# An fp32 kernel of two model blocks on one core: another order and other copies in its up projection, and norm sums in column groups

## What is computed

```
def rms_norm(x, g):
    xf = x.astype(jnp.float32)
    y = xf * lax.rsqrt(jnp.mean(xf * xf, axis=-1, keepdims=True) + EPS)
    return (y * g.astype(jnp.float32)).astype(x.dtype)
...
def conv_ffn(h, w_up, conv_w, w_down):
    a = dwconv_centred(h @ w_up, conv_w)
    val, gate = jnp.split(a, 2, axis=-1)
    return (val * jax.nn.silu(gate)) @ w_down
```

## Time and profile before

| what | value |
|---|---|
| median of 3 runs | 2653.74 us (2653.2 to 2656.26) |
| the profiled execution | 2656.84 us |
| its span | 2655.0 us |
| TensorE, matmuls | 2576.1 us, 97% |
| VectorE | 1068.6 us, 40% |
| ScalarE | 571.6 us, 22% |
| GpSimd | 176.3 us, 7% |
| up stage of layer 0 | from 1744.09 us on |
| up stage of layer 1 | from 2410.60 us on |

### The profile page before, as it was taken

The page is one execution under the profiler, slowest core; times in us unless marked ns, Lnnn a source line. Parts: engine busy times, 40 slices in busy tenths (PEclk is TensorE's granted clock), DMA queues, the critical chain, the costliest instruction groups (busy, mean ns, idle before and its releaser), DMA issues.

```text
span 2655.0 us, 31317 instructions
## 1 busy us (share of the span) xinstructions
PE 2576.1 (97%) x12702; PEld 1862.7 (70%) x12702; DVE 1068.6 (40%) x1883; ACT 571.6 (22%) x1105; POOL 176.3 (7%) x138
## 2 busy tenths in 40 slices
PE   7999999999999899899999999999999999998999
PEld 3556656656666577666886444778886687888998
DVE  2245365364464613254126111146664014115961
ACT  3122222122121112143124100121111013112211
POOL 0000000000000100000000000022120000003410
PEclk9999999999999999999999999999999999999999
DMA  8443343343323043212420222133233232344662
GB/s 313 159 163 133 115 142 112 131 163 116 126 96 111 29 122 95 62 40 73 111 90 7 64 63 63 64 96 95 80 102 88 65 80 64 110 143 129 174 173 66
DMA packets 319738, 280.58 MB, mean 106 GB/s; under 512 B 27618, under 2 KB 298602, under 8 KB 319514
## 3 DMA queue, kind: packets, MB, share of 16 engines
q1 hardware_dynamic: 317882, 274.89, 33.7%
q0 software_dynamic: 1280, 4.20, 0.4%
q10 hardware_dynamic: 479, 0.13, 0.0%
HBM read 278.15 MB, written 1.05 MB: 105 GB/s over the span
## 4 chain that ended last, share of the span: by engine, by line
PE 89%; DVE 7%; ACT 2%; issue 1%; DMA 1%; SPq 1%; ACTq 0%; DVEq 0%
PE ps L683 17%; PE ps L1254 11%; PE ps L1185 9%; PE ps L1323 4%; PE ps L692 4%; PE ps L1313 4%; PE ps L730 4%; PE ps L1197 3%; PE ps L1221 3%; PE ps L449 2%; PE ps L879 2%; PE ps L830 2%; PE ps L812 2%; DVE arena L2085 2%; PE ps L396 2%; PE ps L1034 2%
## 5 line engine op out<-in xcount | busy, mean ns | idle before, releaser
L683 PE MATMUL ps<-hT,ring_mem 128*128 128x512 f32 x1024 | 455.5, 598 | 1.7 <-ACT hT L462 1.7
L683 PEld LDWEIGHTS ps<-hT,ring_mem 128*128 128x128 f32 x1024 | 191.1, 191 | 234.8 <-issue 232.2
L1185 PE MATMUL ps<-hT,ring_mem 128*128 128x512 f32 (+1 forms) x768 | 250.3, 486 | 0.0
L1185 PEld LDWEIGHTS ps<-hT,ring_mem 128*128 128x128 f32 x768 | 145.9, 190 | 101.3 <-issue 91.4
L1254 PE MATMUL ps<-arena 128*128 128x256 f32 (+1 forms) x704 | 132.9, 333 | 12.4 <-DVE arena L2044 12.4
L2016 DVE TENSOR_TENSOR arena<-ps,arena 128x512 f32<-128x512 f32 (+1 forms) x48 | 26.8, 558 | 291.3 <-PE ps L1197 291.3
L730 PEld LDWEIGHTS ps<-arena,K_c 128*128 128x128 f32 x896 | 117.4, 196 | 32.6 <-issue 20.1
L1254 PE MATMUL ps<-hT,arena 128*128 128x256 f32 (+1 forms) x704 | 131.5, 330 | 0.0
L730 PE MATMUL ps<-arena,K_c 128*128 128x128 f32 x896 | 121.4, 291 | 7.4 <-ACT K_c L1467 7.4
L1254 PEld LDWEIGHTS ps<-arena 128*128 128x128 f32 x704 | 112.0, 195 | 22.4 <-issue 13.0
L1254 PE MATMUL ps<-hT,ring_mem 128*128 128x256 f32 (+1 forms) x704 | 123.6, 329 | 2.8 <-DMA ring_mem<-in_w_up_dram 2.8
...
## 6 DMA issues: line engine op xcount, KB each, us to landing
...
ring_mem<-in_hg_w_out_dram SPq DMA_DIRECT2D x8, 1024.0 KB, 12.1
```

The lines of the kernel that those rows point to most:

```text
L683: mm = PE.matmul(bank, wj[:, k, m * 128:m * 128 + 128], hT[:, k, :], start=k == 0, stop=k == 7)
L1185: mm = PE.matmul(ps[:, j, 0:n], wj[:, k, m * 128:m * 128 + 128], hT[:, k, c0:T], start=k == 0, stop=k == 7)
```

## The change

1. **Norm sums in column groups.** For thirteen norms `quarters_tensor` takes the place of `norm_tensor`: eight matmuls with a 128 x 32 matrix of ones, tile k into PSUM partitions 32 x (k mod 4) on. ScalarE copies the four partial sums to `root`, and `whole_tensor`, one matmul with the 128 x 128 matrix of ones some matmuls later, adds them (the factor under the root is 32 instead of 1, since each partial sum stands there 32 times).
2. **Two banks a strip.** The seven products of a strip share two banks: P2 is written where P1 was, P4 where P7 was, and P3 where P5 was, each after ScalarE has copied the earlier one out. Four strips can be in PSUM. ScalarE makes all these copies: P1, P7, P2, P5 (`up_first_scalar`, `seventh`, `second`, `fifth`).
3. **Another order on each engine.** TensorE: P1, P7, P2, P4, P5, P6, P3 in each strip; at the stage's start P1 of four strips around the norm sum, then P2 of four, then the rest in pairs. VectorE: `first_sum(f+1)`, `conv(f-1)`, `hidden(f-2)`, `gather(f)`, and gather has five operations, three of them with both inputs in SBUF.
4. **Weight sums.** VectorE makes one sum a strip instead of two, GpSimd three instead of two; the third is written in place in the ring.
5. **Slots.** Strip f lies in slot (f + 2) mod 4, so strips 0 and 1 lie in the words that the stage `out` doesn't use.
6. Banks of the stages around it are exchanged (`down` begins in banks 4 to 7), and one small operation of layer 1 (`nsink`) is left out.

```diff
...
+        QUARTERED = ["hg_post_a", "mla_pre_a", "hg_post_b", "mix0_a", "mla_post", "mix0_b", "ffn0_a", "ffn0_b", "mix1_a", "mix1_b",
+                     "ffn1_a", "ffn1_b", "final_a"]
+
...
+            if name in QUARTERED:
+                act.wait_ge(quarters_summed, QUARTERED.index(name) + 1)
+                act.wait_ge(normed, sq_base[name])
+                S.activation(root[:, at:at + n], stat(name, n), ACT.Copy).then_inc(quarters_kept, 1)
             act.wait_ge(stat_summed, norm_no[name] + 1)
             if norm_no[name]:
                 act.wait_ge(normed, sq_base[name])
-            S.activation(root[:, at:at + n], stat(name, n), ACT.Sqrt, bias=eps, scale=8.0 / k_n).then_inc(root_ready, 1)
+            S.activation(root[:, at:at + n], stat(name, n), ACT.Sqrt, bias=eps, scale=32.0 if name in QUARTERED else 8.0 / k_n).then_inc(root_ready, 1)
+
+        def quarters_tensor(pe, name, sq, n):
+
+
+            pe.wait_ge(root_ready, norm_no[name])
+            for k in range(8):
+                pe.wait_ge(squared, sq_base[name] + k + 1)
+                c = k % 4 * 32
+                mm = PE.matmul(stat(name, n)[c:c + 32, :], ones[:, 0:32], sq(k), start=k < 4, stop=k >= 4)
+            mm.then_inc(quarters_summed, 1)
+
+        def whole_tensor(pe, name, n, at=0):
+            pe.wait_ge(quarters_kept, QUARTERED.index(name) + 1)
+            PE.matmul(stat(name, n), ones, root[:, at:at + n], start=True, stop=True).then_inc(stat_summed, 1)
 
         def norm_tensor(pe, name, sq, ones_, n):
             k_n = dict(NORMS)[name]
@@ -491,7 +516,7 @@
         mod_mem = ring_mem[:, 8192:12288].rearrange("p (k n) -> p k n", k=4)
...
+            def first(f):
+                ring.wait_loaded(pe, name, (f + 2) % 4, f // 4)
+                if f >= 4:
+                    pe.wait_ge(u_ready, base + f - 3)
+                elif f >= 2:
+                    pe.wait_ge(x_added, x_part(l, "out", "_b", (1, 5)[f - 2]))
+                product(up_bank(f, 0)[:, 0:hw], up_parts(l, f)[0], hT[:, 0:4, a], ready=lambda k: wait_h(pe, f"ffn{l}_a", k) if f == 0 else None
+                        ).then_inc(p1_full, 1)
+
+            def second(f):
+                if f == 0:
+                    wait_h(pe, f"ffn{l}_a", 7)
+                pe.wait_ge(p1_kept, base + f + 1)
+                product(up_bank(f, 0)[:, 0:hw], up_parts(l, f)[1], hT[:, 4:8, a]).then_inc(p2_full, 1)
+
+            def seventh(f):
+                if f >= 4:
+                    pe.wait_ge(c_ready, base + f - 3)
+                pe.wait_ge(third_sum_ready, base + f + 1)
                 if f == 0:
                     pe.wait_ge(turned_ready, 4 * l + 1)
-                product(f, "P7", sums[:, 2], T_up[:, 0])
-                if f == 0:
-                    pe.wait_ge(turned_ready, 4 * l + 2)
-                product(f, "P5", sums[:, 0], hT[:, 0:4, b])
-                pe.wait_ge(sums_ready, FT * l + f + 1)
-                if f == 0:
-                    pe.wait_ge(turned_ready, 4 * l + 3)
-                product(f, "P6", sums[:, 1], T_up[:, 1])
-                mm = product(f, "P3", sums[:, 3], hT[:, 4:8, b])
+                product(up_bank(f, 1)[:, hw:2 * hw], up_parts(l, f)[2], T_up[:, 0]).then_inc(p7_full, 1)
+
+            def others(f):
+                _, _, _, a22 = up_parts(l, f)
+                pe.wait_ge(p7_kept, base + f + 1)
                 if f == 0:
                     pe.wait_ge(turned_ready, 4 * l + 4)
-                    mm = p4()
-                strip_used(mm)
-
-            plain(0)
+                if f >= 2:
+                    pe.wait_ge(first_sum_ready, (FT - 2) * l + f - 1)
+                product(up_bank(f, 1)[:, hw:2 * hw], a22, T_up[:, 2])
+                product(up_bank(f, 1)[:, 0:hw], S_up[:, f % 2, 0], hT[:, 0:4, b]).then_inc(p5_full, 1)
+                pe.wait_ge(p2_kept, base + f + 1)
+                pe.wait_ge(sums_ready, base + f + 1)
+                product(up_bank(f, 0)[:, hw:2 * hw], S_up[:, f % 2, 1], T_up[:, 1]).then_inc(p6_full, 1)
+                pe.wait_ge(p5_kept, base + f + 1)
+                strip_used(product(up_bank(f, 1)[:, 0:hw], S_up[:, f % 2, 2], hT[:, 4:8, b]))
+
+            first(0)
+            first(1)
             ffn_norm_tensor(pe, l, "_b")
-            for f in range(FT):
-                if f == 0:
-                    plain(1)
-                    pe.wait_ge(root_ready, norm_no[f"ffn{l}_b"] + 1)
-                if f >= 2:
-                    plain(f)
-                summed(f)
+            first(2)
+            first(3)
+            whole_tensor(pe, f"ffn{l}_b", hw, at=hw)
+            for f in range(4):
+                second(f)
+            for f in (0, 2):
+                seventh(f)
+                seventh(f + 1)
+                others(f)
+                others(f + 1)
+            for f in range(4, FT):
+                first(f)
...
+
+            def second(f):
+                act.wait_ge(p2_full, base + f + 1)
+                if f >= 2:
+                    act.wait_ge(conv_ready, base + f - 1)
+                S.activation(C_up[f % 2][:, 0:hw], up_bank(f, 0)[:, 0:hw], ACT.Copy).then_inc(p2_kept, 1)
...
             for f in range(FT):
-                act.wait_ge(strips_used, ring.stages[f"up{l}"]["first"] + f + 1)
-                S.activation(P1_up[:, 0:n // 2], up_region(f, "P1", n // 2), ACT.Copy).then_inc(p1_kept, 1)
-                act.wait_ge(c_ready, FT * l + f + 1)
+                if f >= 4:
+                    up_first_scalar(act, l, f)
+                if f >= 1:
+                    taps(f - 1)
+                if f >= 4 or f % 2 == 0:
+                    seventh(f)
+                if f < 4 and f % 2 == 0:
+                    seventh(f + 1)
+                second(f)
                 if f >= 2:
-                    act.wait_ge(hid_ready, raised(FT * l + f - 1))
-                for part in range(2):
-                    S.activation(acc[:, f % 2 * 2 + part, 0:n], C_up[f % 2][:, part, 0:n], ACT.Identity,
-                                 scale=tap(l, 1, f, part)).then_inc(tap_ready, 1)
-                if f:
-                    gate(f - 1)
...
+            def first_sum(f):
+
+
+                _, _, a21, a22 = up_parts(l, f)
+                wait_strip_f(dve, l, f - 2)
+                ring.wait_loaded(dve, f"up{l}", (f + 2) % 4, f // 4)
+                V.tensor_tensor(S_up[:, f % 2, 0], a21, a22, ALU.add).then_inc(first_sum_ready, 1)
+
             def gather(f):
-                P = lambda which: up_region(f, which, hw)
-                U = lambda i: U_up[:, i, 0:hw]
-                C = C_up[f % 2]
-                dve.wait_ge(strips_used, ring.stages[f"up{l}"]["first"] + f + 1)
-                dve.wait_ge(p1_kept, FT * l + f + 1)
-                if f >= 2:
-                    dve.wait_ge(tap_ready, 2 * (FT * l + f - 1))
-                st.mark(V.tensor_tensor(U(0), P1_up[:, 0:hw], P("P6"), ALU.add))
-                V.tensor_tensor(C[:, 0, 0:hw], P1_up[:, 0:hw], P("P2"), ALU.add)
+                C, U, P57 = C_up[f % 2], P1_up[:, f % 4, 0:hw], P57_up[f % 2]
+                both = view(C, (hw, 2), (1, hw), at=hw)
+                dve.wait_ge(p1_kept, base + f + 1)
+                dve.wait_ge(p2_kept, base + f + 1)
+                V.tensor_tensor(C[:, 0:hw], C[:, 0:hw], U, ALU.add)
+                dve.wait_ge(p6_full, base + f + 1)
+                V.tensor_tensor(U, U, up_bank(f, 0)[:, hw:n], ALU.add).then_inc(u_ready, 1)
+                dve.wait_ge(u_ready, base + f + 1)
+                dve.wait_ge(p7_kept, base + f + 1)
+                dve.wait_ge(p5_kept, base + f + 1)
+                st.link(V.tensor_tensor(both, view(U, (0, 2), (1, hw)), view(P57, (hw, 2), (1, hw)), ALU.add))
+                st.mark(V.tensor_tensor(C[:, n + hw:2 * n], C[:, n:n + hw], P57[:, 0:hw], ALU.add))
+                wait_strip_f(dve, l, f)
                 st.settle()
-                st.mark(V.tensor_tensor(U(1), U(0), P("P7"), ALU.add))
-                st.mark(V.tensor_tensor(U(2), U(0), P("P5"), ALU.add))
-                st.settle()
...
+            for f in range(FT):
+                if 1 <= f < FT - 1:
+                    first_sum(f + 1)
+                if f >= 1:
                     conv(f - 1)
                 if f >= 2:
                     hidden(f - 2)
+                gather(f)
+            conv(FT - 1)
+            hidden(FT - 2)
+            hidden(FT - 1)
 
...
                 pool.wait_ge(y_ready, raised(8 * l + 8))
                 for f in range(FT):
-                    t, j = divmod(f, 4)
-                    ring.wait_loaded(pool, f"up{l}", j, t)
+                    ring.wait_loaded(pool, f"up{l}", (f + 2) % 4, f // 4)
                     sums = S_up[:, f % 2]
                     a11, a12, a21, a22 = up_parts(l, f)
                     if f >= 2:
-                        pool.wait_ge(first_sums_ready, (FT - 2) * l + f - 1)
+                        pool.wait_ge(first_sum_ready, (FT - 2) * l + f - 1)
```

(6 more changed lines are left out.)

222 lines of the change are left out of this document (124 added, 98 removed).

## The result

The changed kernel takes 2672.32 us (median of 4 runs, 2670.55 to 2674.73) against 2654.79 us (2653.2 to 2656.26) for the kernel before, measured beside it: ratio 1.0065, 95% interval 1.005 to 1.0079. The profiled execution's span is 2672.8 us against 2655.0.

The account below looks back on a forecast made before the run. TensorE, busy 97%, was taken as the bound, with VectorE nearly so in layer 1's up stage. Terms -12.8 - 3.2 + 35 = +19 gave 2673 us as a median; range 2642 to 2696, from the terms' bounds 2656 to 2696.

Parts of the forecast that it names:

- Turn of layer 1: Layer 1's up stage, steady state: a strip takes 8.0 us instead of 6.25, TensorE waiting 1.75 us in each; +33 over the strips.
- Its mechanism: VectorE operations with two SBUF inputs advance at about 21% of their speed while GpSimd runs its sums.
- rival 3: Full exclusion in layer 1's up stage: multiply-adds do nothing beside GpSimd, a turn of 8.7 us, total 2686 us; chance 0.15.
- Rival 1: GpSimd steals less or lies elsewhere: VectorE never slowed, a turn of 5.2 us, stage TensorE-bound, total 2626 us; chance 0.17.
- Start of layer 1: Start of layer 1's up stage: new waits 11.2 and 5 for the clock, against 11.3 and 0.9 that go; +4.
- Clock in the steady state: Layer 1's up stage: the clock may fall after waits of 1.75 us, TensorE's slack taking most up; +2 (0 to 13).
- End: End of layer 1's up stage: VectorE's backlog gone, so waits of 2.11 and 0.5 and 1.7 us of lower clock go; -4.3.
- Layer 0: Start of layer 0's up stage: shorter wait for turned tiles, new waits for the third sum; net -3.2 us (-6 to 0).
- Norms: Thirteen norms' sums of squares in column groups: 2.09 us saved per full norm; -12.8 us in sum, between -16 and -8.
- Rivals 1 and 2: Rival 1, and a second: half as much lost in layer 1's up stage (40% speed), total 2657 us; the second's chance 0.10.
- rival 4: Norms' column groups run one after another: +0.43 instead of -2.09 us a norm, total 2691 us; chance 0.03.

## Why the prediction was right, step by step

**Turn of layer 1: right.** 8.0 us forecast, 8.05 measured; from the first wait for L1728 to the last one, 2579.56 - 2442.57 = 137.0 us for 17 strips, 30.7 more than 17 x 6.25, against 29.8 forecast. The four multiply-adds "at 4 us and more": 4.56. The wait for L1728: 1.53. The first longer wait: 3.30, forecast 3.5. GpSimd busy 51.50 of 100 us.

**Its mechanism: right in the operations and the size, wrong in form.** The prediction spread the loss as a speed of 21% under GpSimd. In truth each GpSimd sum holds one VectorE operation. Multiply-adds one by one show it; this is the answer for line L2189 of the changed kernel (duration of one in ns, lowest, median, highest):

```profile
L2189 DVE SCALAR_TENSOR_TENSOR arena<-K_c,vecs,arena x24: 471/1362/1489, 2458.6 to 2543.1; 128x255 f32<-128x255 f32 x24
```

Three of four last about as long as a sum, the fourth its own 0.47 us. The kernel before had it already; asked for one by one between 2458 and 2544 us, its multiply-adds are not all a little slow. In the strip of the earlier trace rows the first takes 1.26 us, beside GpSimd's second sum, and the other three 0.47 to 0.48:

```profile
L2085 DVE SCALAR_TENSOR_TENSOR arena<-K_c,vecs,arena x28: 471/482/1268, 2457.4 to 2536.0; 128x255 f32<-128x255 f32 x28
```

That the two forms agree on the turn rests on the shape of this row of work; with halved sums, 8.1 to 8.3 us by the 21% against 7.82 measured, they don't. The Trainium skill (SBUF — State Buffer, "Summary: rules for kernel authors") says that where VectorE has two SBUF inputs and GpSimd reads SBUF, the second to issue "fully blocks until the first finishes". These rows agree with it, operation by operation. What rival 3 took from that rule, that VectorE does nothing at all while GpSimd has sums to make (8.7 us, 2686), doesn't follow: between two sums one VectorE operation gets in. (Rival 1's turn adds up to 5.3 us and not 5.2 with the 1.79 us of the earlier trace rows for the multiply-adds; nothing hangs on it.)

**Start of layer 1: too dear.** +4 forecast. The stage took 2583.23 - 2396.23 = 187.0 us against 152.5 before, +34.6; less 30.7 and 3.3 this leaves +0.6. The waits were 2.35, 1.69 and 5.22 (forecast 2.4, 2.4, 5.2), the small ones of 1.2 didn't come, and the lower clock cost about 2.5 us and not 5: 0.9 after the first wait, 1.6 after the third, none after the second.

**Clock in the steady state: +2 forecast, nothing came.** Behind the first longer wait, 3.30 us, the clock did fall (0.50 from 2444.60 to 2446.60), and three products took 2446.98 - 2442.57 = 4.41 us instead of 2.68; but TensorE's slack took it up, for the next strip's wait was missing (no gap before 2450.60). After waits of 1.5 to 1.7 us in every strip the granted clock was 1.00 from 2450 to 2550. The term was taken from a single wait of 2.11 us.

**End: right.** -4.3 forecast; layer 1's first half of down took 38.0 us instead of 42.3.

**Layer 0: right.** -3.2 forecast, -2.7 in the trace (275.8 against 278.5 us), with the waits of 1.39, 3.41 and 0.91 us where 1.4, 3.1 to 3.5 and 1.0 stood.

**Norms: over.** -12.8 forecast, -10.8 by the traces, -8 by the runs. The groups took 1.00 us and not 0.93, so a norm saves 2.0 us and not 2.09; four norms from mix0_a to ffn0_a brought 7.3 us for the 8.4 forecast. Block one gave back all of its norms' savings: its last waited stretch ends at 1037.63 instead of 1036.43, and 1.06 of these 1.2 us were there before the first norm (943.04 against 944.10, a difference between the two executions ahead of anything the change touches). The forecast had -0.7 there, with +2 for the clock. Two waits, 0.91 and 0.82 us in the kernel before, grew by 1.7 us each, and the matmuls behind them ran slower (5.38 and 5.81 us against 3.69 and 5.23):

```profile
1005.39 5.38 PE L883 MATMUL ps<-hT,ring_mem 128*128 128x256 f32 x16 [2.62 <-issue]
...
1018.40 5.81 PE L421 MATMUL ps<-hT,ones 128*128 128x256 f32 x16 [2.55 <-DVE xT L1944]
```

**The sum.** In the traces -10.8 - 2.7 + 30.3 (34.6 - 4.3) + 1.1 = +17.9 us, measured +17.8. Forecast -12.8 - 3.2 + 35 = +19. Both large terms were a few us too large, and these errors went against each other: by the runs -8 and +25, against -12.8 and +32. So the deciding term was right, but that the total came out within 1 us was in part luck. Why the traces give the norms -10.8 and the runs -8 isn't settled: the traces are one execution each, and the interval of the run with groups alone, -11 to -5 us, holds both; and in the profiled execution with plain sums the clock happened to stay up behind the wait of 3.40 us in layer 0, where the changed kernel lost 1.6 us. Rivals 1 and 2 fell with the 8.05 us, rival 4 with the 1.00 us.
